# RWKV time mixing on one core: the next head pair's projections between the steps over the present pair's blocks, its last norm and new sample state beside the next pair's levels

## The chip, the cores and the metric

The kernel runs on one core of a Trainium2 chip. The metric is device time in microseconds, the median of several executions. Its core has TensorE (PE, with its weight load written PEld), VectorE (DVE), ScalarE (ACT), GpSimd (POOL) and SyncE (SP), which here issues most DMAs.

## The reference

One inference step of a two-layer trunk: an RWKV-7 layer and a convolution layer, each followed by an expert retrieval, over 512 prompt tokens and 8 samples of 8 tokens (576 columns together), width 1024, all in float32. The change is in the RWKV layer, which has 16 heads of 64 (shortened):

```python
r, k, v = jnp.einsum('ibtd,ide->ibte', xm[:3], w_rkv)
decay = jnp.exp(-jnp.exp(w));  a = jax.nn.sigmoid(a0 + (xa @ a1) @ a2);  g = jax.nn.sigmoid(xg @ g1) @ g2
kk = k * k_k;  kk = kk / jnp.maximum(jnp.sqrt(jnp.sum(kk * kk, -1, keepdims=True)), 1e-12)
def step(S, inp):
    r_t, w_t, k_t, v_t, kk_t, a_t = inp
    sa = jnp.einsum('bhij,bhj->bhi', S, -kk_t)
    S = S * w_t[:, :, None, :] + sa[..., None] * (kk_t * a_t)[:, :, None, :] + v_t[..., None] * k_t[:, :, None, :]
    return S, jnp.einsum('bhij,bhj->bhi', S, r_t)
s_fin, y = lax.scan(step, s0, xs)
yn = (y - mean) * lax.rsqrt(var + GN_EPS) * ln_w + ln_b
out = ((yn + bonus) * g) @ w_o
```

## The kernel before

The RWKV layer runs in `wkv`, a loop over C = 8 pairs of heads (i = 0 to 7, 128 channels each), with the tokens along the free axis: 4 blocks of 128 prompt tokens and 64 sample tokens. The order of each engine's instructions is written out by hand; the engines meet at counting semaphores (`Steps` gives the value at which a named step is done). A pair goes through four stages:

1. **Projections** (PE lines 418 to 440). The decay `w` and the rate `a` (expansions of hidden rows with the small weights `low2`, L412), the products for `k`, `r` and `v` with the weights in `K.w[0]`, `K.w[1]`, `K.w[2]` (L406, 16 matmuls of 288 columns each), sums for the key norm, the gate `g`, the bonus, and transposes of v, b and k to token rows (`tok_v`, `tok_b`, `tok_k`, L439). ACT evicts (L626 to L648); DVE makes the logs of decay (L704 to L715), the norm's reciprocal (L724) and the four factors at, rt, bt, kt (L730 to L735).
2. **Grams** (L447 and L465, masks on DVE L744 to L751): products of the factors within each block.
3. **Levels** (L478 to L505): the inverse of a triangular matrix of each block by six doublings. In each level PE turns the present inverse (`turn`), multiplies (`y`) and makes the correction (`dXT`); ACT evicts, and DVE adds (`XT`, L759; at the last level L761). POOL makes the factors `co` (L852) and `XT_sides` (L856).
4. **Steps** over the four blocks: for block b the rows R (L514, L517), U (L526), outputs Y (L531 to L537), state update S (L539, L540), with `update_state` on DVE (L765 to L772). Between them stand the small products of the samples (L566, L571, L547 to L559, L587, L590, L598 to L607). Then the **tail**: `mean` (L412), the samples' new state `s_S` (L615) and `var` (L412). DVE then makes the samples' new state (L819 to L823, step name `s_state`) and the last norm (reciprocal of `sd` L825, to the output rows `y` L834), in front of the next pair's logs.

SP's queue is one list as well. For each pair it loads the weights of k, r and v as their buffers come free (L372), `low2` (L374, shown by the trace as in_low) and the columns `prm` (L377), then stores the prompt's state (L382), waits for `s_state`, stores the samples' state from `s_state` (L386), waits for those stores to land and loads the next pair's into the same tile (L360):

```python
                sp.wait_ge(dve_s.sem, dve_s.before("s_state", i))
                for e in range(2):
                    q = slice(64 * e, 64 * e + 64)
                    sp.dma_start(I["o_wkv_s"][bass.ds(i - 1, 1), q].squeeze(0), s_state[q, :, q]).then_inc(stored, 16)
                sp.wait_ge(stored, i * 64 + 64)
                load_state(i)
```

After `wkv` comes `retrieval_and_conv`, the rest of the program; its first work is the product with `w_o` (L1211) whose result DVE adds to the residual `K.x` (L1607).

Of the kernel before, what the change touches and what calls it, by code (L numbers as in the profile page):

```python
# [35 lines left out]
LEVELS = 7  # L36
SLEVELS = 3
# [215 lines left out]
def wkv(nc, K, I, xm, y_out, hid_wa, hid_g, R, wo_loaded):  # L253

# [22 lines left out]
    sc = R.cut(3 * NB + SB)
    esc = R.cut(3 * NB + SB)
# [3 lines left out]
    R.cut(2, NB, HD)  # L282
    R.cut(P)
# [15 lines left out]
    Q = Region(K.arena, R.at)
    s_state = Q.cut(SB, P)  # L300
# [6 lines left out]
    Q3 = Region(K.arena, g_at)  # L307
    uv_exp = Q3.cut(SB, P)
    s_prod = Q3.cut(SB, P)
# [3 lines left out]
    stored, zeroed = K.sem("wkv_stored"), K.sem("wkv_zeroed")  # L313
    pe_s = Steps(K.sem("wkv_pe"),
                 ["w", "k", "a", "r", "norm", "v", "g", "bonus", "tok_v", "tok_b", "tok_k"]
                 + [f"gram_{x}{e}" for x in ("L", "LT", "G", "RB", "RK") for e in range(2)]
                 + [f"{x}{l}_{e}" for l in range(1, LEVELS) for step in (("turn", "y"), ("dXT",)) for e in range(2) for x in step]
                 + ["R0", "s_tok", "s_gram0", "s_gram1", "U0", "Y0", "S0"]
                 + ["s_y1", "R1", "s_d1", "U1", "Y1", "S1"]
                 + ["s_y2", "R2", "s_d2", "U2", "Y2", "S2"]  # L320
# [30 lines left out]
    with nc.Block() as block:  # L351
        @block.sync
        def _(sp):
            sp.sem_inc(stored, 64)
            weight = (1, 0, 2)

            def load_state(i):
# [1546 lines left out]
```

## Time and profile before

| | us |
|---|---|
| median of 3 runs (lowest, highest) | 3976.35 (3967.84, 3978.03) |
| the profiled execution's own time | 3980.32 |
| its span in the trace | 3978.5 |
| PE busy in the span | 2955.1 (74%) |
| DVE busy | 2732.4 (69%) |
| ACT busy | 1470.4 (37%) |
| mean granted clock of TensorE | 0.853 of full |

All times in the trace count from the span's start. A float32 matmul shows as two records, so 16 matmuls are "x32". A timeline row gives start, duration, engine, line, operation, tiles, shape, count and in brackets the engine's idle time before it with what ended it. "In pair n" below counts from 0.

### The profile page before, as it was taken

The page shows a single profiled execution, that of the slowest core. Times are in us where ns is not written, and L with a number is a line of the kernel's source. Part 1 is how long each engine was busy: PE and PEld are TensorE (multiplying, and loading weights), DVE is VectorE, ACT ScalarE, POOL GpSimd, SP SyncE. Part 2 cuts the span into 40 slices and gives each one's busy share as a digit, 9 for nine tenths or more (in the row PEclk, how much of TensorE's full clock was granted, in tenths as well). Part 3 has the DMA queues.
Part 4 walks back from the last instruction along what each step waited for, and adds up shares of the span by engine and source line. Part 5 has one row for each costly group of instructions (what it writes and reads, how often), then busy time and mean ns, then how long its engine had stood idle before and what let it go on. Part 6 is the DMA issues. An engine that isn't in the chain of part 4 may idle for free.

```text
span 3978.5 us, 56287 instructions
## 1 busy us (share of the span) xinstructions
PE 2955.1 (74%) x20248; PEld 1449.0 (36%) x20248; DVE 2732.4 (69%) x6352; ACT 1470.4 (37%) x4424; POOL 1424.2 (36%) x1272
## 2 busy tenths in 40 slices
PE   5999999868766666777777766788787676666655
PEld 3777777754222122333333322334342222222111
DVE  5555555546766666778777777889867677777775
ACT  1333333313433333444444433444444343333333
POOL 0001110014444444344444444334444444444442
PEclk8888999889787778888889888999998787787777
DMA  2110000039999999999999999999999999999996
GB/s 79 30 30 26 25 25 25 18 111 425 426 426 427 426 427 426 421 416 399 411 404 426 426 426 425 415 353 369 421 394 427 426 425 427 426 426 426 426 426 289
DMA packets 229640, 1311.06 MB, mean 330 GB/s; under 512 B 58736, under 2 KB 61936, under 8 KB 81648
## 3 DMA queue, kind: packets, MB, share of 16 engines
q0 software_dynamic: 165888, 1208.03, 72.6%
q1 hardware_dynamic: 63472, 99.43, 7.1%
q8 instruction: 159, 2.61, 0.3%
q14 instruction: 121, 0.99, 0.1%
HBM read 1301.52 MB, written 5.86 MB: 329 GB/s over the span
## 4 chain that ended last, share of the span: by engine, by line
DMA 36%; PE 19%; DVE 16%; ACT 3%; issue 3%; DVEq 1%; POOL 1%; ACTq 1%; POOLq 0%
DMA arena<-in_uv,arena 36%; DVE arena L1587 8%; PE psum L1159 8%; PE psum L1121 4%; PE psum L1211 3%; PE psum L1241 2%; DVE arena L1674 1%; POOL arena L1101 1%; ACT wbuf L1377 1%; PE psum L1231 1%; ACT arena L1372 1%; DVE arena L1515 1%; DVE arena L1512 0%; ACT arena L1368 0%; DVE arena L1648 0%
## 5 line engine op out<-in xcount | busy, mean ns | idle before, releaser
L1159 PE MATMUL psum<-arena,wbuf 64*64 64x512 f32 (+1 forms) x8704 | 1451.1, 741 | 865.7 <-ACT wbuf L1377 846.3
L1101 POOL DMA_INDIRECT arena<-in_uv,arena x1152 | 1349.7, 1172 | 1770.7 <-PE psum L1159 1569.4
L1587 DVE SCALAR_TENSOR_TENSOR arena<-arena 128x1024 f32<-128x1024 f32 x1152 | 1396.0, 1222 | 584.9 <-DMA arena<-in_uv,arena 569.6
L1159 PEld LDWEIGHTS psum<-arena,wbuf 64*64 64x64 f32 (+1 forms) x8704 | 335.0, 154 | 1755.5 <-ACT wbuf L1377 1379.3
L1368 ACT ACTIVATE arena<-arena 128x2 f32<-128x2 f32 x576 | 117.0, 203 | 1668.1 <-DVE arena L1587 1663.4
L1377 ACT ACTIVATE wbuf<-cst,arena 128x64 f32<-128x64 f32 x1152 | 338.3, 340 | 41.6 <-issue 2.4
L1121 PE MATMUL psum<-arena,wbuf 128*128 128x256 f32 (+1 forms) x1024 | 312.4, 453 | 8.5 <-DVE arena L1598 5.8
L1372 ACT ACTIVATE arena<-arena 128x1 f32<-128x1 f32 x1152 | 276.8, 287 | 40.9 <-issue 1.4
L1121 PEld LDWEIGHTS psum<-arena,wbuf 128*128 128x128 f32 x1024 | 203.9, 210 | 171.5 <-issue 131.2
L842 POOL COPY arena<-arena 128x256 f32<-128x256 f32 x8 | 3.2, 397 | 584.2 <-DVE arena L735 584.2
L406 PE MATMUL psum<-arena,wbuf 128*128 128x288 f32 x768 | 193.6, 411 | 0.4 <-DMA wbuf<-in_w_rkv 0.4
L406 PEld LDWEIGHTS psum<-arena,wbuf 128*128 128x128 f32 x768 | 145.7, 191 | 46.2 <-ACT arena L628 3.1
L1674 DVE SCALAR_TENSOR_TENSOR arena<-arena,par 128x256 f32<-128x256 f32 x240 | 115.6, 482 | 48.3 <-ACT arena L1433 42.3
L1368 ACT ACT_TABLE_LOAD x105 | 134.7, 1283 | 21.6 <-DVE arena L1587 20.0
L1231 PE MATMUL psum<-arena 128*128 128x256 f32 (+1 forms) x512 | 137.3, 415 | 0.0
L1211 PE MATMUL psum<-arena 128*128 128x320 f32 (+1 forms) x384 | 113.3, 439 | 15.6 <-ACT arena L1445 14.9
L1241 PE MATMUL psum<-arena 64*64 64x256 f32 x1024 | 121.1, 387 | 0.0
L1231 PEld LDWEIGHTS psum<-arena 128*128 128x128 f32 x512 | 93.8, 190 | 58.5 <-issue 36.5
L1358 ACT ACT_TABLE_LOAD x79 | 101.4, 1283 | 4.4 <-issue 0.3
L1211 PEld LDWEIGHTS psum<-arena 128*128 128x128 f32 x384 | 72.2, 197 | 71.2 <-issue 35.0
L1587 DVE DVE_READ_ACCUMULATOR arena<-arena 128x1 f32 x1152 | 94.3, 82 | 0.0
L1241 PEld LDWEIGHTS psum<-arena 64*64 64x64 f32 x1024 | 71.7, 137 | 55.1 <-issue 21.7
(264 smaller groups left out, 3322.9 us busy)
## 6 DMA issues: line engine op xcount, KB each, us to landing
wbuf<-in_w_q SPq DMA_DIRECT2D x64, 576.0 KB, 11.8
arena<-in_w_pw SPq DMA_DIRECT2D x48, 512.0 KB, 8.7
arena<-in_uv,arena POOLq DMA_INDIRECT x1152, 20.3
wbuf<-in_w_rkv SPq DMA_DIRECT2D x24, 512.0 KB, 3.6
wbuf<-in_w_o SPq DMA_DIRECT2D x8, 512.0 KB, 3.7
arena<-in_w_o SPq DMA_DIRECT2D x8, 512.0 KB, 8.5
x<-in_x SPq DMA_DIRECT2D x1, 2304.0 KB, 8.2
arena<-in_state SPq DMA_DIRECT2D x16, 128.0 KB, 3.0
```

Source lines behind the costliest of these rows:

```text
L406: last = pe.matmul(ps[:, bank + h, 0:HALF], w[:, k, :], src[:, k, h * HALF:(h + 1) * HALF], start=k == 0, stop=k == C - 1)
L1101: pool.indirect_dma_start(ring[:, g % RING, :], None, I["uv"][p // 2], bass.IndirectOffsetOnAxis(ap=idx[:, s % 4, j:j + 1], axis=0)).then_ ...
L1121: last = pe.matmul(ps[:, 7, 0:WIDTH[half]], K.w9[j][:, k, :], h[half][:, k, :], start=k == 0, stop=k == C - 1)
L1159: last = pe.matmul(ps[e * HD:(e + 1) * HD, 2 * (u % 2) + a if u < NB else 4, :], diag[t, g % DIAGS, :], ring[t, g % RING, D + e * 512:D + ...
L1211: last = pe.matmul(ps[:, BANK[c % 2], 0:WIDTH[half]], weights[c % 2][:, k, :], src[:, k, :], start=k == 0, stop=k == C - 1)
L1231: last = pe.matmul(out, wb[j][:, k, :], h[half][:, k, :], start=k == 0, stop=k == C - 1)
L1241: last = pe.matmul(part[q], tap_diags[q, k, :], ups[c % 2][q, k:k + 2 * P], start=k == 0, stop=k == PE_TAPS - 1)
L1368: act.activation(gelu[:, q], dots[:, q], ACT.Gelu)
L1372: act.activation(coef[:, c:c + 1], gelu[:, c:c + 1], ACT.Copy, scale=share[:, s % 4, j + k:j + k + 1])
L1377: act.activation(diag[:, (g + k) % DIAGS, :], K.ident2, ACT.Copy, scale=coef[:, c:c + 1]).then_inc(diag_ready, 1)
L1587: stt(out=row, in0=row, scalar=1.0, in1=tok[p % 2][:, UNITS[p % 2].index(u), :], op0=ALU.mult, op1=ALU.mult, accum_out=dots[:, g % COLS:g ...
L1674: last = stt(out=out, in0=up[:, k:k + 2 * P], scalar=K.par[:, TAP0 + k, c:c + 1], in1=out, op0=ALU.mult, op1=ALU.add)
```

## The change

The program's order changes in five ways; what is computed stays the same.

- PE: projections become a generator `front(n)` of 52 pieces (two of `w` and `a` together, one half of the tokens each; 48 single matmuls of k, r, v; two norm sums). Pair 0's run ahead of the loop; those of pair i+1 are handed out by `fill(count)` between the steps of pair i. All use banks 2 and 3, half by half, so evictions on ACT are split in halves too. The transposes to token rows move into levels 1 to 3.
- ACT and DVE: the next pair's evictions, exponentials, logs, rated key, norm reciprocal (in four pieces of 144 columns), bonus terms and factors stand between the present pair's steps.
- DVE: the last norm of pair i-1 and then its samples' new state are ten pieces, two of them behind each of levels 1 to 5 of pair i.
- SP: pair by pair the loads for pair i+1 (weights, `prm`, `low2`), the prompt state's store, the wait for `s_state` of pair i, the samples' store, and the load of the next samples' state.
- Several work tiles move into `K.x`; so the input x is loaded again at the end, six eighths behind the last `s_state` and two eighths behind the last `y`; the first product of the next stage waits for it.

```diff
+            for i in range(C):
+                if i < C - 1:
+                    for j, name in enumerate(("k1", "r1", "v1")):
+                        sp.wait_ge(pe_s.sem, pe_s.value(f"{name}.{i}"))
+                        sp.dma_start(K.w[j], I["w_rkv"][3 * (i + 1) + weight[j]]).then_inc(wl[j], 16)
+                    sp.wait_ge(act_s.sem, act_s.value(f"k1.{i}"))
+                    sp.wait_ge(dve_s.sem, dve_s.value(f"rk.{i}"))
+                    sp.dma_start(prm, I["cpar"][i + 1]).then_inc(prm_loaded, 16)
+                    sp.wait_ge(pe_s.sem, pe_s.value(f"g.{i}"))
+                    sp.dma_start(low2, I["low2"][i + 1]).then_inc(low_loaded, 16)
+                else:
+                    for j, name in enumerate(("k1", "r1")):
+                        sp.wait_ge(pe_s.sem, pe_s.value(f"{name}.{i}"))
+                        sp.dma_start(K.w[j], I["w_o"][j]).then_inc(wo_loaded[j], 16)
+                sp.wait_ge(dve_s.sem, dve_s.value(f"state{NB - 1}.{i}"))
...
+                sp.wait_ge(dve_s.sem, dve_s.value(f"s_state.{i}"))
+                if i == C - 1:
+                    sp.dma_start(K.x[:, 0:X_EARLY, :], I["x"][:, 0:X_EARLY, :]).then_inc(x_back, 16)
                 for e in range(2):
-                    q = slice(64 * e, 64 * e + 64)
...
+                if i < C - 1:
+                    sp.wait_ge(s_stored, i * 32 + 32)
+                    load_state(i + 1)
+            sp.wait_ge(dve_s.sem, dve_s.value(f"y.{C - 1}"))
+            sp.dma_start(K.x[:, X_EARLY:C, :], I["x"][:, X_EARLY:C, :]).then_inc(x_back, 16)
+            sp.wait_ge(p_stored, C * 32)
+            sp.wait_ge(s_stored, C * 32)
```

```diff
+            def front(n):
+
+                pe.wait_ge(low_loaded, n * 16 + 16)
                 for h in range(2):
-                    for k in range(C):
-                        last = pe.matmul(ps[:, bank + h, 0:HALF], w[:, k, :], src[:, k, h * HALF:(h + 1) * HALF],
-                                         start=k == 0, stop=k == C - 1)
-                last.then_inc(pe_s.at(name), 1)
-
-            def expand(w, src, bank, name):
+                    if h:
+                        pe.wait_ge(act_s.sem, act_s.value(f"a0.{n}"))
+                    elif n:
+                        pe.wait_ge(act_s.sem, act_s.value(f"tok_k.{n - 1}"))
+                        pe.wait_ge(dve_s.sem, dve_s.value(f"XT{LEVELS - 1}_0.{n - 1}"))
+                    pe.matmul(ps[:, 2, 0:HALF], low2[0:HD, 0, :], hid_wa[0:HD, of_half(h)], start=True, stop=True)
+                    pe.matmul(ps[:, 3, 0:HALF], low2[HD:P, 0, :], hid_wa[HD:P, of_half(h)], start=True,
+                              stop=True).then_inc(pe_s.at(f"wa{h}.{n}"), 1)
+                    yield
+                pe.wait_ge(wl[0], n * 16 + 16)
+                pe.wait_ge(act_s.sem, act_s.value(f"a1.{n}"))
                 for h in range(2):
-                    last = pe.matmul(ps[:, bank + h, 0:HALF], w, src[:, h * HALF:(h + 1) * HALF], start=True, stop=True)
-                last.then_inc(pe_s.at(name), 1)
-
+                    yield from project(n, xm[1], 0, h, "k")
+                pe.wait_ge(wl[1], n * 16 + 16)
+                pe.wait_ge(act_s.sem, act_s.value(f"k0.{n}"))
+                yield from project(n, xm[0], 1, 0, "r")
+                pe.wait_ge(act_s.sem, act_s.value(f"k1.{n}"))
...
+                yield from project(n, xm[2], 2, 0, "v")
+                pe.wait_ge(act_s.sem, act_s.value(f"r1.{n}"))
+                yield from project(n, xm[2], 2, 1, "v")
+
```

```diff
+                fill(1)
+                pe.wait_ge(act_s.sem, act_s.value(f"tok_k.{i}"))
+                pe.wait_ge(dve_s.sem, dve_s.value(f"XT{LEVELS - 1}_1.{i}"))
...
                         if j == 4:
-                            last.then_inc(pe_s.at(f"s_gram{e}"), 1)
+                            last.then_inc(pe_s.at(f"s_gram{e}.{i}"), 1)
+                fill(1)
                 rows_U(0)
+                fill(2)
                 rows_Y_S(0)
-                for b in (1, 2):
...
-                    rows_Y_S(b)
-
+                fill(6)
+                sample_y(1)
+                rows_R(1)
...
-                pe.wait_ge(act_s.sem, act_s.value("s_U", i))
-                pe.nop(nofuse=True)
+                fill(4)
+                pe.wait_ge(act_s.sem, act_s.value(f"s_U.{i}"))
                 pe.matmul(ps[:, 4, 0:NS], s_rows[NS:P, :], K.ident[NS:P, NS:P], start=True, stop=False)
```

```diff
+            def new_sample_state(i):
+                tt(s_state, s_state, s_prod, ALU.add)
+                yield
+                dve.drain()
+                tt(s_state, s_state, unsq(esc[:, i % 2, 3 * NB:3 * NB + SB], 2, P), ALU.mult).then_inc(dve_s.at(f"s_state.{i}"), 1)
+
+            def last_norm(i):
+
+                dve.wait_ge(act_s.sem, act_s.value(f"sd.{i}"))
+                for part in range(4):
+                    reciprocal(sd, part)
+                    yield
+                dve.drain()
+                tt(yc, yc, sd, ALU.mult)
+                yield
+                dve.drain()
+                ts(yc, yc, ln[:, i % 2, 0:1], ln[:, i % 2, 1:2], ALU.mult, ALU.add)
+                yield
+                dve.drain()
+                tt(yc, yc, bon[i % 2], ALU.add)
+                yield
+                dve.drain()
+                for y, t in zip(y_out, (slice(0, T // 2), slice(T // 2, N))):
+                    last = tt(y[:, i, :], yc[:, t], g_s[i % 2][:, t], ALU.mult)
+                last.then_inc(dve_s.at(f"y.{i}"), 1)
+                yield
+                yield from new_sample_state(i)
...
                         else:
-                            dve.tensor_copy(XT[0:HD, e, :, HD:P], by_block(ps[0:HD, 4 * e + 2, 0:NB * HD])).then_inc(dve_s.at(f"XT{l}_{e}"), 1)
+                            dve.tensor_copy(XT[0:HD, e, :, HD:P], by_block(ps[0:HD, 4 * e + 2, 0:NB * HD])).then_inc(dve_s.at(f"XT{l}_{e}.{i}"), 1)
+                    if l < LEVELS - 1:
+                        next(behind, None)
+                        next(behind, None)
...
+                    if n == "wA" and c in (0, X_EARLY):
+                        dve.wait_ge(x_back, 16 if c == 0 else 32)
                     dst = K.x[:, c, cols(half)]
```

On PE, the end of the levels and the start of the steps, before. L505 is the last level's `dXT`, L514 and L517 R, L566 and L571 the samples' transposes and grams, L526 U, L531 the first of Y:

```order
L505 MATMUL psum<-arena 64x64 x8
L514 MATMUL psum<-arena 128x128
L517 MATMUL psum<-arena 128x64 x2
L566 MATMUL psum<-cst,arena 128x128 x2
L571 MATMUL psum<-arena 64x64 x10
L526 MATMUL psum<-arena 128x64 x2
L531 MATMUL psum<-arena 128x128
```

The same place in pair 0 of the changed kernel. L420 and L421 are the next pair's `w` and `a`, L403 its projection matmuls, L544 the last `dXT`, L551 and L554 R, L603 and L608 the samples', L563 U, L568 the first of Y:

```order
L544 MATMUL psum<-arena 64x64 x8
L420 MATMUL psum<-arena 128x288
L421 MATMUL psum<-arena 128x288
L551 MATMUL psum<-x,arena 128x128
L554 MATMUL psum<-arena 128x64 x2
L603 MATMUL psum<-cst,x 128x128 x2
L608 MATMUL psum<-arena 64x64 x10
L420 MATMUL psum<-arena 128x288
L421 MATMUL psum<-arena 128x288
L563 MATMUL psum<-x,arena 128x64 x2
L403 MATMUL psum<-arena,wbuf 128x288 x2
L568 MATMUL psum<-arena,x 128x128
```

The next pair's first piece now stands ahead of R; behind U come the first two of its 48 projection matmuls, which before followed the whole tail.

On SP, one round of the loop before, from a pair's last loads to the next ones; in brackets the semaphores that an issue waits for:

```order
L377 DMA arena<-in_cpar 128x55 [waits wkv_dve,wkv_act]
L382 DMA out_o_wkv_p<-arena 64x64 [waits wkv_dve]
L386 DMA out_o_wkv_s<-arena 512x1x64 [waits wkv_dve]
L360 DMA arena<-in_state 64x8x64 [waits wkv_stored]
L372 DMA wbuf<-in_w_rkv 128x1024 [waits wkv_pe] x3
L374 DMA arena<-in_low 128x256 [waits wkv_pe]
```

And in the changed kernel:

```order
L376 DMA arena<-in_low 128x256 [waits wkv_pe]
L384 DMA out_o_wkv_p<-arena 64x64 [waits wkv_dve]
L390 DMA out_o_wkv_s<-arena 512x1x64 [waits wkv_dve]
L359 DMA arena<-in_state 64x8x64 [waits wkv_s_stored]
L371 DMA wbuf<-in_w_rkv 128x1024 [waits wkv_pe] x3
L374 DMA arena<-in_cpar 128x55 [waits wkv_dve,wkv_act]
L376 DMA arena<-in_low 128x256 [waits wkv_pe]
```

The order of kinds is nearly the same; the wait in front of out_o_wkv_s (`s_state` of the pair before) now ends at level 5 of the present pair, and the rows behind it carry the loads for the pair after the present one, `low2` last.

On DVE, the changed kernel's levels of pair 1. L923 is the addition `XT` of a level, L836 a quarter of the reciprocal, L874 to L884 the rest of the last norm of pair 0, L862 and L865 its samples' new state, L925 the last level's copy:

```order
L923 TENSOR_TENSOR arena<-arena,psum 128x64x2 x2
L836 RECIPROCAL x<-x 128x144 x2
L923 TENSOR_TENSOR arena<-arena,psum 128x32x4 x2
L923 TENSOR_TENSOR arena<-arena,psum 128x16x8 x2
L874 TENSOR_TENSOR x<-x 128x576
L877 TENSOR_SCALAR x<-x,arena 128x576
L880 TENSOR_TENSOR x<-x 128x576
L884 TENSOR_TENSOR arena<-x,arena 128x256
L884 TENSOR_TENSOR arena<-x,arena 128x320
L862 TENSOR_TENSOR arena<-arena,x 128x1024
L865 TENSOR_TENSOR arena<-arena 128x1024
L925 COPY arena<-psum 64x4x64 x2
```

Before, these pieces stood in one run (L821 to L834) behind the tail, beside the next pair's first projections.

## Rows read from the trace of the kernel before

**Rows 1.** Windows: stretch, length, busy PE PEld DVE ACT POOL, PEclk, DMA share, GB/s.
```profile
438.00:527.00 89.00, 80.65 (x964) 64.39 (x962) 48.59 (x95) 29.17 (x64) 9.27 (x14) 0.92 0.10 27
```

**Rows 2.** Timeline of PE, one period of the loop.
```profile
396.36 0.68 PE L478 MATMUL psum<-cst,arena 64*64 64x64 f32 x16 [0.67 <-DVE arena L751]
...
414.12 0.49 PE L514 MATMUL psum<-arena 128*128 128x128 f32 x2 [0.51 <-DVE arena L761]
...
435.80 0.41 PE L598 MATMUL psum<-arena 64*64 64x64 f32 x4 [1.94 <-DVE arena L806]
...
446.54 1.36 PE L412 MATMUL psum<-arena,cst 128*128 128x288 f32 x4
...
449.00 8.03 PE L406 MATMUL psum<-arena,wbuf 128*128 128x288 f32 x32
...
478.85 1.09 PE L439 MATMUL psum<-cst,arena 128*128 128x128 f32 x8 [1.59 <-DVE arena L735]
479.87 1.63 PE L447 MATMUL psum<-arena 64*64 64x64 f32 x80
...
485.05 0.68 PE L478 MATMUL psum<-cst,arena 64*64 64x64 f32 x16 [0.67 <-DVE arena L751]
```

**Rows 3.** Windows of 2 us, columns as in rows 1.
```profile
442.00:444.00 2.00, 2.00 (x5) 1.06 (x5) 0.87 (x2) 0.00 (x0) 0.00 (x0) 0.50 0.00 0
...
464.00:466.00 2.00, 2.00 (x10) 1.53 (x9) 0.00 (x0) 0.00 (x0) 0.00 (x0) 1.00 0.00 0
```

**Rows 4.** Timeline of SP, the end of a pair and the next pair's loads.
```profile
450.71 1.23 SPq L386 DMA_DIRECT2D out_o_wkv_s<-arena  x2
453.99 1.26 SPq L360 DMA_DIRECT2D arena<-in_state  x2
457.06 18.18 SPq L372 DMA_DIRECT2D wbuf<-in_w_rkv  x3
```

**Rows 5.** Timeline of SP, the first loads of the stage.
```profile
80.24 0.33 SPq L362 DMA_DIRECT2D arena<-in_low  x1
...
81.09 1.38 SPq L365 DMA_DIRECT2D wbuf<-in_w_rkv  x3
```

**Rows 6.** DMA view of 85 to 108 us, in 40 slices: tenths busy.
```profile
DMA  9999930000000000005778000000000010749800
```

**Rows 7.** Timeline of PE, start of the stage.
```profile
82.32 2.28 PE L412 MATMUL psum<-arena 64*128 64x288 f32 x4 [3.09 <-DMA arena<-in_low]
84.97 9.80 PE L406 MATMUL psum<-arena,wbuf 128*128 128x288 f32 x32 [0.37 <-DMA wbuf<-in_w_rkv]
```

**Rows 8.** Timeline of DVE, levels and tail.
```profile
401.84 0.29 DVE L759 TENSOR_TENSOR arena<-arena,psum 128x128 f32<-128x128 f32 x1 [2.05 <-PE psum L501]
...
413.07 0.42 DVE L761 COPY arena<-psum 64x256 f32<-64x256 f32 x1 [1.63 <-PE psum L505]
...
448.15 1.23 DVE L821 TENSOR_TENSOR arena<-arena 128x1024 f32<-128x1024 f32 x1
...
450.59 3.75 DVE L825 RECIPROCAL arena<-arena 128x576 f32<-128x576 f32 x1
```

**Rows 9.** Timeline of ACT, a table load and the work behind it.
```profile
449.15 1.28 ACT L626 ACT_TABLE_LOAD   x1 [0.47 <-PE psum L412]
450.45 0.74 ACT L626 ACTIVATE arena<-psum,arena 128x576 f32<-128x576 f32 x1
```

**Rows 10.** Timeline of PE, last pair and what follows it.
```profile
767.18 0.49 PE L514 MATMUL psum<-arena 128*128 128x128 f32 x2 [0.51 <-DVE arena L761]
...
803.10 1.13 PE L412 MATMUL psum<-arena,cst 128*128 128x288 f32 x4
814.40 9.44 PE L1211 MATMUL psum<-arena,wbuf 128*128 128x256 f32 x32 [10.17 <-PEq L351]
```

**Rows 11.** Source line L514: duration ns min/median/max, first and last start us, forms.
```profile
L514 PE MATMUL psum<-arena x64: 275/377/581, 140.5 to 789.1; 128*128 128x128 f32 x64
```

**Rows 12.** Page, DMA issues: queue, KB, us to landing.
```profile
x<-in_x SPq DMA_DIRECT2D x1, 2304.0 KB, 8.2
```

More of the change, by code:

```diff
@@ L311, in wkv @@
+    yc, ysq = Q3.cut(N), Q3.cut(N)
+    sd, s_prod = ysq, s_pick
     wl = [K.sem(f"wkv_w{j}") for j in range(3)]
     low_loaded, prm_loaded, state_loaded = (K.sem(f"wkv_{x}_loaded") for x in ("low", "prm", "state"))
[L313 to L320, printed above, removed]
-                 + ["s_RT", "R3", "U3", "s_U", "Y3", "S3"]
-                 + ["s_Y", "mean", "s_S", "var"], a_pass_ahead=True)
@@ new lines, in wkv @@
+    dve_s = Steps(K.sem("wkv_dve"), passes("logs kf kk rk factors",
+                  ["bonus"] + [f"{x}{e}" for x in ("maskLT", "level0_") for e in range(2)]
+                  + [f"gram{x}{e}" for x in ("G", "RB", "RK") for e in range(2)]
+                  + [f"XT{l}_{e}" for l in range(1, LEVELS - 2) for e in range(2)] + ["-y"]
+                  + [f"XT{LEVELS - 2}_{e}" for e in range(2)] + ["-s_state"] + [f"XT{LEVELS - 1}_{e}" for e in range(2)]
+                  + "s_gram state0 +logs s_X1 state1 +kf s_X2 state2 s_RT state3 +kk s_y s_exp +rk yc +factors s_prod".split()))
@@ L336, in wkv @@
+    pool_s = Steps(K.sem("wkv_pool"), passes("", ["s_copies"]
+                   + [f"co{l}_{e}" for l in range(1, LEVELS - 1) for e in range(2)] + ["XT_sides"]))
     assert NB == 4 and SLEVELS == 3
@@ L609, in _ @@
[L609 to L612 removed]
+                last.then_inc(pe_s.at(f"s_Y.{i}"), 1)
+                fill(4)
+                pe.wait_ge(dve_s.sem, dve_s.value(f"s_y.{i}"))
+                pe.wait_ge(act_s.sem, act_s.value(f"Y.{i}"))
+                for h in range(2):
+                    last = pe.matmul(ps[:, h, 0:HALF], K.headones, y_s[:, of_half(h)], start=True, stop=True)
@@ L613, in _ @@
+                last.then_inc(pe_s.at(f"mean.{i}"), 1)
+                for _ in ahead:
+                    pass
+                pe.wait_ge(dve_s.sem, dve_s.value(f"s_exp.{i}"))
                 for h in range(2):
@@ L693, in _ @@
+                act.wait_ge(pe_s.sem, pe_s.value(f"var.{i}"))
+                act.activation(halves(sd), of_banks(ps, 0), ACT.Sqrt, bias=K.eps[:, 1:2], scale=1.0 / HD).then_inc(act_s.at(f"sd.{i}"), 1)
         @block.vector
         def _(dve):
-            dve_s.begin(dve)
             tt, ts, stt = dve.tensor_tensor, dve.tensor_scalar, dve.scalar_tensor_tensor
@@ new lines, in _ @@
+            logs(0)
+            rated_key(0)
+            norm_floor(0)
+            for part in range(4):
+                reciprocal(nrm, part)
+            unit_key(0)
+            bonus_terms(0)
+            dve.drain()
+            make_factors(0)
+            for i in range(C):
+                n, more = i + 1, i < C - 1
+                behind = last_norm(i - 1) if i else iter(())
+                dve.wait_ge(act_s.sem, act_s.value(f"v1.{i}"))
+                dve.wait_ge(pe_s.sem, pe_s.value(f"bonus.{i}"))
+                tt(halves(bon[i % 2]), of_banks(ps, 2), halves(v_s), ALU.mult).then_inc(dve_s.at(f"bonus.{i}"), 1)
@@ L837, in _ @@
+            for _ in last_norm(C - 1):
+                pass
         @block.gpsimd
```

653 lines of the change are left out of this document (356 added, 297 removed).

## The prediction

> **What bounds the kernel now.** Read the windows by period first. In a stretch of 89 us [rows 1] TensorE is busy 80.65, VectorE 48.59, ScalarE 29.17: while `wkv` runs, PE sets the pace and no other engine is near. The rest of the program, from 814.40 on [rows 10], the change leaves alone; it is worth its old time, later or earlier by what `wkv` gives. So only the eight pairs matter.
>
> Then PE's timeline over one period [rows 2]. Levels begin at 396.36, the first R at 414.12, `var` at 446.54, and the next pair's levels at 485.05: 88.7 us, as 17.8 of levels, 33.7 of steps and tail (414.12 to about 447.8, where `var` ends and the next `w` begins), 37.2 of projections and grams. Two things cost time without PE working. First, waits: between the first R and `var` PE's timeline shows six gaps before an instruction, 0.3 to 1.94 us, 5.4 us together, the longest for the samples' rows [rows 2]; the projections' end waits 1.59 for the factors [rows 2]. Second, the clock: where projections run the granted clock is 1.00, in the tail 0.50, which is 1.2 GHz [rows 3]. In the windows of this period, 2 us each (two of 45 are shown), it is low from about 426.2 to 429.6 and 436.9 to 447.0, 13.5 us, less 1.1 us of gap. At 2.4 GHz that work takes half, 6.2 us less. So the steps' own PE work at full clock is 33.7 - 5.4 - 6.2 = 22.1 us.
>
> **The change, part by part.** I add up one period of pairs 1 to 6.
>
> Projections filled in. The three products take 8.03 us each for 16 matmuls [rows 2], 0.50 each; 24.1. Two norm sums of the same width are 1.0. The `w` and `a` pairs have 64 rows each in different halves of the array: 1.2 if they overlap, 2.3 if not; I take 1.7. Together 26.8. All of it now stands between the steps. Can the steps hide it all from waits? I walked the list with row durations. Before each thing that PE waits for stands a fill of 3 to 6 matmuls, 1.5 to 3 us, and the evictions and `update_state` (three instructions of about 0.35) take 0.3 to 1.2. For the samples' rows PE waited 1.94 behind R and U [rows 2]; now six fills, 3.0 us, stand there too. Exposed are only: `w` and `a` on ScalarE at the start, where half 1 of the expansion waits for half 0's eviction and k for both, about 1.0 with one table load (below), and 0.5 before `mean` and at the next pair, where DVE's list (uv_exp, bonus terms, then five factor products) is tightest. Steps and tail: 22.1 + 26.8 + 1.5 = 50.4. Bounds 48.5 (overlap, no wait) and 52.5 (one more microsecond of each).
>
> The table load is 1.28, and the activation behind it starts 1.30 after it [rows 9]; so a switch costs 1.3 here. The Trainium skill ("ScalarE: Activation LUTs", What ACT_TABLE_LOAD costs) says that a switch to another set takes about 2.66 us, a drain of 1.38 included. By that, an estimate, the first wait of each steps stage would be 1.4 longer, and the whole some 10 us slower; the trace disagrees, with no such gap before the activation.
>
> Gate, bonus and grams. 1.0 + 1.0 + the stretch from L447 to the levels, 485.05 - 479.87 = 5.2 [rows 2], + 0.3 of waiting for `s_prod`: 7.5.
>
> Levels. 17.1 from 396.36 to where DVE's copy L761 ends, 413.07 + 0.42 [rows 2, 8]. Plus the three transposes, 0.5 each, 1.5. Plus DVE's pieces: each level leaves it 2.05 idle [rows 8]. A quarter of the 3.75 reciprocal [rows 8] is 0.94, two are 1.9; the next pairs of pieces are 1.5 and 1.75; these fit. Behind level 5 stand two passes of 1024 columns, 1.23 each [rows 8], 2.6 with the drain between, in a gap of 1.63 [rows 8]: 1.0 longer. Sum 19.6.
>
> SP's queue, the new wait. This is the term that decides. In the order of SP, the loads of weights, `prm` and `low2` for pair i+1 stand behind the samples' store and load, and these behind `s_state` of pair i-1, which DVE now makes behind level 5 of pair i. Call that moment S. The store is issued at once and the state load follows 3.28 later (450.71 to 453.99, [rows 4]), as it waits for landing; two issues take 1.26 [rows 4]; so the first weights go out at S + 4.6. At the start of the stage three weights go out from 81.09 [rows 5], and the queue is busy until 88.05 (five and a third slices of 0.575 from 85, [rows 6]), the state's 256 KB included: 6.96 us. Now the state's bytes lead and `low2` ends the queue, so it lands near S + 11.5. PE's `front` asks for it right behind the last level, when DVE has made the first copy, S + 0.6. PE therefore stands 10.9 us, with R, U and everything of the steps queued behind the waiting instruction; ACT stands before `prm` as well. If `low2` didn't queue behind the weights it would need only its own issue, S + 6.5, and the 2.1 from 80.24 to the first matmul at 82.32 [rows 5, 7]: 8.0 us of stall. Upper bound 11.4. The case occurs for i = 1 to 6; pair 0 has no `s_state` ahead of its loads, pair 7 no next pair.
>
> The clock after the stall. At the start of the stage PE had waited 3.09; its first expansion took 2.28 and k 9.80 [rows 7] against 8.03 at full clock [rows 2]: 1.1 + 1.8 = 2.9 lost. Here the first microseconds hold waits for ACT anyway, so I take 2.2, bounds 0 and 4.0.
>
> Sum per period: 50.4 + 7.5 + 19.6 + 10.9 + 2.2 = 90.6, where before had 88.7. Without the last two terms it would be 77.5.
>
> The whole. Pair 0's R began at 140.5 [rows 11]. Its projections lose about 1.5 to finer waits and save the 1.6 and the transposes; the transposes return in the levels: 141.2. Steps of pair 0 without stall: 191.6. Six periods: 543.6, so 735.2. Pair 7: 7.5 + 19.6 + 0.6 to its R, 762.9, before 767.18 [rows 10]. Its steps have no fills: 33.7 as in rows 2, or 37.0 as pair 7 took (767.18 to 803.10 + 1.13, [rows 10]); 35.3 gives 798.2, before 804.2.
>
> Then the end. Before, PE went on at 814.40 [rows 10], 10.2 behind `var`, when DVE was through the last norm. Now that norm no longer waits for the samples' state and ends 8.2 behind `var` (0.9 for `sd`, 3.9 for the reciprocal, 3.4 for five further passes), `s_state` follows 2.6 later, and only then SP sends six eighths of x, 1.77 MB, ahead of the samples' store whose landing closes the stage. The whole x took 8.2 [rows 12]; six eighths about 6.7. With the store behind it some 8.6: 19.4 behind `var`, 9.2 more than before. So the next stage begins at 817.6 instead of 814.4: 3.2 on top of the profiled execution's own 3980.32 (span 3978.5), or 0.1%. That execution lies 4 above the median 3976.35 of the runs, so the median to expect is 3979.5, which I give as 3979: **no change that can be told**. I call 0.3%, 12 us, the bound of that.
>
> **The rivals.**
> 1. *A shorter stall.* `low2` and k's weights land early, 8.0 instead of 10.9, and the clock is back sooner (1.0 lost): -4.1 x 6 = -25, 3954. For it: most loads land in 3.6 us alone. Against: the start shows three weights filling the queue for 7 us [rows 5, 6]. It also stands for steps at their low bound, 48.5: -13.
> 2. *No stall*, as if the loads were early enough: 77.5 a period, -79, 3900. It takes SP to pass a wait that stands in its list; nothing speaks for that but a slip of my reading.
> 3. *Slower: the clock stays at 1.2 GHz.* After each stall the steps stage begins with its thinnest PE work, and before, a low stretch lasted from 436.9 to 447.0 though PE was busy [rows 3]. Each further microsecond at half clock in the filled steps costs 0.5. Up to 6 us low is in my sum; it decides from 9 us low on (1.5 x 6 = 9, with the 3 above), and at 12 us gives +18, 3997. Against: k reached full clock within a few us at the start [rows 7]. The Trainium skill ("TensorE: Matmul & The Clock Gate", Why this matters for your kernels) has it that idle gaps between bursts send the array back to half rate, and steady work restores it; it speaks for the loss after each of the six stalls, and not for a longer one.
>
> **How the numbers follow.** Forecast case 0.42; rival 1 0.24; rival 2 0.08; rival 3, with DVE or ACT chains that run over, 0.26. Per period the bounds (8.0 to 11.4, 48.5 to 52.5, 0 to 4.0) would together give -42 to +26 us; eight in ten I put at 3936 to 4001, leaving out rival 2 and the far ends. Faster by over 0.3%: rivals 1 and 2, 0.32. Slower by over 0.3%: rival 3 and the forecast's upper edge, 0.29. Within: 0.39.
>
> **What would show it.** In the changed kernel's trace: PE idle about 11 us before L420 in pairs 1 to 6, ended by the load of in_low, and no such gap in pair 0; granted clock 0.5 right behind it; then a steps stage of 50 us nearly without gaps at 1.00; SP's weights issued 4.6 behind L865; some 9 us more between last `var` and the first product of the next stage. The prediction fails if that gap is under 8 us, if the filled steps take over 53, or if the clock falls within them.

## The result, and the profile after the change

| us | before | after |
|---|---|---|
| median of 10 runs (lowest, highest) | 3974.70 (3967.84, 3978.03) | 3981.18 (3978.09, 3987.98) |
| span of the profiled execution | 3978.5 | 3978.4 |
| PE, DVE, ACT busy in it | 2955.1, 2732.4, 1470.4 | 2913.3, 2732.4, 1471.2 |
| mean granted clock | 0.853 | 0.859 |

After over before is 1.0019, 95% interval 1.0011 to 1.0028: 0.2% slower. That is within the 0.3% called no change, and 3981 is 2 us from the 3979 forecast. The step itself is 6.5 us where 3.2 were forecast, but so small a step says little: the median of the kernel before was 3976.6 and 3978.2 when it was measured again beside the experiments. The order of a whole stage has changed and the sum has not. Two things must be shown: what the fills saved, and what took it back.

Start with how often a pair comes round. SP stores the prompt's state once a pair. Its timeline in the changed kernel (start, duration, queue and line):

```profile
181.34 1.18 SPq L384 DMA_DIRECT2D out_o_wkv_p<-arena  x2
...
722.68 1.16 SPq L384 DMA_DIRECT2D out_o_wkv_p<-arena  x2
```

From first to last are six periods, (722.68 - 181.34) / 6 = 90.22 us, of the forecast 90.6. The window of one period (columns as in [rows 1]):

```profile
438.00:527.00 89.00, 75.11 (x960) 59.85 (x959) 48.51 (x101) 27.94 (x68) 10.19 (x14) 0.92 0.10 27
```

PE is now busy 75.11 of 89 where it was 80.65 [rows 1], with nearly the same number of matmuls (960 records for 964) and the same mean clock of 0.92. So there is a hole of some 12 us, part of the low clock lies in it, and what work there is goes faster. PE's timeline of one period, which answers to [rows 2], shows it. L544 is the last level's `dXT`, L420 the next pair's `w`, L403 its products, L472 the gate, L508 the start of the levels, L457 transposes to token rows:

```profile
396.11 1.25 PE L544 MATMUL psum<-arena 64*64 64x64 f32 x16
409.65 0.84 PE L420 MATMUL psum<-arena 64*128 64x288 f32 x1 [12.29 <-DMA arena<-in_low]
...
416.49 2.26 PE L403 MATMUL psum<-arena,wbuf 128*128 128x288 f32 x4
...
462.49 1.13 PE L472 MATMUL psum<-arena 128*128 128x288 f32 x4
...
469.54 0.68 PE L508 MATMUL psum<-cst,arena 64*64 64x64 f32 x16 [0.51 <-DVE arena L914]
...
471.53 0.66 PE L457 MATMUL psum<-cst,arena 128*128 128x128 f32 x4
...
475.15 0.66 PE L457 MATMUL psum<-cst,arena 128*128 128x128 f32 x4
...
487.65 1.25 PE L544 MATMUL psum<-arena 64*64 64x64 f32 x16
501.48 0.84 PE L420 MATMUL psum<-arena 64*128 64x288 f32 x1 [12.58 <-DMA arena<-in_low]
```

One gap of 12.29 us between the end of the levels and the first piece of the next projections, ended by the load of low2. The steps after it have 48 projection matmuls among them and up to the gate one wait, of 0.30. The view of waits, 82 to 830 us (engine, line, what was waited for: total, times, longest), says how often:

```profile
PE psum L420 <- DMA arena<-in_low: 78.1, 7, 12.9
```

Seven times: 3.00 at the start of the stage, then once for each of pairs 1 to 6, 75.1 us in all, 12.5 each. What low2 waited for stands in SP's timeline, the answer to [rows 4]:

```profile
397.91 1.23 SPq L390 DMA_DIRECT2D out_o_wkv_s<-arena  x2
401.16 1.26 SPq L359 DMA_DIRECT2D arena<-in_state  x2
402.47 1.57 SPq L371 DMA_DIRECT2D wbuf<-in_w_rkv  x3
404.13 0.38 SPq L374 DMA_DIRECT2D arena<-in_cpar  x1
404.55 0.60 SPq L376 DMA_DIRECT2D arena<-in_low  x1
```

and in DVE's, at the same place (L865 is the second pass of the samples' new state, step `s_state`; L925 the last level's copies):

```profile
396.40 1.48 DVE L865 TENSOR_TENSOR arena<-arena 128x1024 f32<-128x1024 f32 x1
397.81 0.73 DVE L925 COPY arena<-psum 64x256 f32<-64x256 f32 x2
```

`s_state` is done at 396.40 + 1.48 = 397.88 and SP's store goes out at 397.91. Store, wait for landing, state load, then three weights, `prm`, and low2 as the last at 404.55. All of that is for a pair whose first matmul was due at 398. PE starts at 409.65.

The clock behind the gap, in windows of 2 us as in [rows 3]:

```profile
402.00:404.00 2.00, 0.00 (x0) 0.00 (x0) 0.00 (x0) 0.00 (x0) 0.00 (x0) 0.50 0.53 120
...
418.00:420.00 2.00, 2.00 (x12) 1.40 (x10) 0.00 (x0) 0.00 (x0) 0.00 (x0) 0.50 0.00 0
430.00:432.00 2.00, 2.00 (x14) 1.64 (x11) 0.99 (x3) 0.18 (x1) 0.00 (x0) 1.00 0.00 0
```

0.50 of full, which is 1.2 GHz, from within the gap to 420, and then 1.00 through steps and tail, where before it was 0.50 for 13.5 us. The six pairs are not alike in this. In windows of 1 us the clock is low until 4 to 6 us behind the first `w` in four of them, and until 10.4 behind it in two, the one shown here and the one that starts at 590.63.

The end of `wkv`, PE and then SP, as in [rows 10]:

```profile
796.73 1.13 PE L675 MATMUL psum<-x,cst 128*128 128x288 f32 x4
817.24 9.87 PE L1377 MATMUL psum<-arena,wbuf 128*128 128x256 f32 x32 [19.38 <-PEq L351]
```

```profile
808.15 0.33 SPq L387 DMA_DIRECT2D x<-in_x  x1
808.53 1.68 SPq L390 DMA_DIRECT2D out_o_wkv_s<-arena  x2
```

19.38 idle behind `var` instead of 10.17; x is reloaded behind the last samples' state, and the store stands behind that load (experiment 3 tests it). Of the pairs' gain nothing is left there either: the next stage starts at 817.24, 2.8 later than before.

### The profile page after: what moved, and what is told of

The parts are those of the page before. It is cut to its first block, busy times and chain, and to the rows that moved or that the text cites. A ratio compares the mean times of both kernels' runs of the same rounds, so it can differ in the third digit from the quotient of the medians.

```text
span 3978.4 us, 56329 instructions
## 1 busy us (share of the span) xinstructions
PE 2913.3 (73%) x20248; PEld 1416.6 (36%) x20248; DVE 2732.4 (69%) x6400; ACT 1471.2 (37%) x4472; POOL 1413.2 (36%) x1272
## 4 chain that ended last, share of the span: by engine, by line
DMA 35%; PE 18%; DVE 17%; ACT 3%; issue 3%; DVEq 1%; POOL 1%; ACTq 1%; POOLq 0%
DMA arena<-in_uv,arena 35%; DVE arena L1753 9%; PE psum L1325 8%; PE psum L1377 3%; PE psum L1287 3%; PE psum L1407 2%; DVE arena L1842 1%; POOL arena L1267 1%; ACT wbuf L1543 1%; PE psum L1397 1%; ACT arena L1538 1%; DVE arena L1681 1%; DVE arena L1678 1%; DVE arena L1685 0%; DVE level L1707 0%
## 5 line engine op out<-in xcount | busy, mean ns | idle before, releaser
L1267 POOL DMA_INDIRECT arena<-in_uv,arena x1152 | 1333.0, 1157 | 1785.2 <-PE psum L1325 1578.3
L1287 PE MATMUL psum<-arena,wbuf 128*128 128x256 f32 (+1 forms) x1024 | 304.4, 444 | 8.4 <-DVE arena L1764 5.8
L1287 PEld LDWEIGHTS psum<-arena,wbuf 128*128 128x128 f32 x1024 | 198.5, 204 | 166.9 <-issue 127.3
L403 PE MATMUL psum<-arena,wbuf 128*128 128x288 f32 x768 | 212.2, 419 | 4.6 <-ACT arena L683 3.6
L403 PEld LDWEIGHTS psum<-arena,wbuf 128*128 128x128 f32 x768 | 141.2, 194 | 41.3 <-issue 5.3
```

Source lines behind the costliest of these rows:

```text
L403: last = pe.matmul(ps[:, 2 + h, 0:HALF], K.w[j][:, k, :], src[:, k, of_half(h)], start=k == 0, stop=k == C - 1)
L1267: pool.indirect_dma_start(ring[:, g % RING, :], None, I["uv"][p // 2], bass.IndirectOffsetOnAxis(ap=idx[:, s % 4, j:j + 1], axis=0)).then_ ...
L1287: last = pe.matmul(ps[:, 7, 0:WIDTH[half]], K.w9[j][:, k, :], h[half][:, k, :], start=k == 0, stop=k == C - 1)
```

## The experiments

Theory A is the forecast's: the fills are worth about 13 us a pair, and SP's list, in which the loads of the next pair stand behind the wait for `s_state`, takes the same back. The main rival B: the order on PE itself is no better, and low2's wait only takes up time that PE, DVE or ACT would lose anyway; without it another wait would come out. Rival C: not the queue's wait but the amount of loads ahead of low2 counts. And for the clock: half clock behind the gap is a cost of its own (D), or hidden by waits for ACT. All kernels compute the reference in full; junk matmuls below are matmuls whose result nobody reads.

**1. The loads ahead of the wait (e1_queue).** SP issues the loads for the pair after next before it waits for `s_state`.

```diff
+            next_loads(0)
+            for i in range(C):
                 sp.wait_ge(dve_s.sem, dve_s.value(f"state{NB - 1}.{i}"))
...
+                if i < C - 1:
+                    next_loads(i + 1)
                 sp.wait_ge(dve_s.sem, dve_s.value(f"s_state.{i}"))
```

> Edit: on SP the loads for pair i+2 (weights, prm, low2) stand ahead of the wait for s_state of pair i, not behind it. Theory A (the queue order makes the six stalls): the six gaps of about 12 us before the expansion of w and a are gone, and with them some 2 us each of half clock; 6 x 13 = 78 us less than the changed kernel's 3981, 3903, ratio to before 0.982. Theory B (the filled steps themselves have eaten the gain, and the gap would only move to another wait): 3970 or more, with a new gap of like size in the steps.

Measured 3906.94 (3897.16 to 3912.35), ratio 0.983 [0.9814, 0.9847]. The same part of SP's timeline:

```profile
333.45 1.15 SPq L387 DMA_DIRECT2D out_o_wkv_p<-arena  x2
334.64 6.63 SPq L371 DMA_DIRECT2D wbuf<-in_w_rkv  x3
...
344.60 0.33 SPq L376 DMA_DIRECT2D arena<-in_low  x1
370.39 1.24 SPq L395 DMA_DIRECT2D out_o_wkv_s<-arena  x2
```

low2 is issued at 344.60, 26 us before it is wanted. PE there:

```profile
370.84 0.82 PE L425 MATMUL psum<-arena 64*128 64x288 f32 x1 [0.99 <-DVE arena L930]
```

The gap before `w` (L425 now) is 0.99, ended by DVE, instead of 12.3 ended by a load. Three of the six periods between prompt stores are 76.65 (180.15, 256.80, 333.45), the others 77.6, 77.6 and 80.2, mean 77.54; the forecast's sum without stall and low clock was 77.5. Before, the mean was 89.3, so the gain is 11.8 a pair, and 12.7 where the clock stays up. The next stage starts at 733.18, 84 earlier; the ratios of the medians show 75 of them, as the profiled execution (3897.16) was the fastest of the four. That is A; B would have kept the time. In the longer periods the clock is what differs. Two windows of the longest, behind the 0.99 gap above:

```profile
370.00:382.00 12.00, 11.12 (x59) 7.99 (x60) 3.85 (x22) 3.79 (x8) 0.85 (x1) 0.57 0.22 44
382.00:394.00 12.00, 12.00 (x74) 9.27 (x72) 6.03 (x18) 2.70 (x9) 0.00 (x0) 1.00 0.01 2
```

12 us at 0.57, with no gap over a microsecond. The window from 260 to 349 us of this kernel, mostly in periods of 76.65, is at 1.00.

**2. Only the order of the loads (e2_small_first).** They stay behind the wait; `prm` and low2 go ahead of the three weights.

```diff
+                    sp.dma_start(prm, I["cpar"][i + 1]).then_inc(prm_loaded, 16)
+                    sp.wait_ge(pe_s.sem, pe_s.value(f"g.{i}"))
+                    sp.dma_start(low2, I["low2"][i + 1]).then_inc(low_loaded, 16)
+                    for j, name in enumerate(("k1", "r1", "v1")):
```

> Edit: only the order of the loads behind s_state is changed: prm and low2 ahead of the three weights. If low2 is late because 1.5 MB of weights stand ahead of it in the queue: it lands near S + 7 instead of S + 11.7, each gap shrinks by 4.5 to 5 us, the k product isn't held up by its weights (they land near S + 10, it is wanted near S + 13), 3981 - 28 = 3953. If the landing is set by the issue alone, weights or not: within 5 us of 3981. If PE then only waits for the weights of k instead: also near 3981, with a gap before the first projection matmul.

3959.86 (3957.92 to 3963.81), ratio 0.9957 [0.9941, 0.9974]. SP and PE:

```profile
393.95 1.23 SPq L390 DMA_DIRECT2D out_o_wkv_s<-arena  x2
...
399.17 0.43 SPq L373 DMA_DIRECT2D arena<-in_low  x1
399.64 1.38 SPq L376 DMA_DIRECT2D wbuf<-in_w_rkv  x3
```

```profile
402.19 0.84 PE L420 MATMUL psum<-arena 64*128 64x288 f32 x1 [8.79 <-DMA arena<-in_low]
...
409.03 1.30 PE L403 MATMUL psum<-arena,wbuf 128*128 128x288 f32 x2
```

In this pair low2 goes out 5.2 behind `s_state` instead of 6.7, and PE starts 8.2 behind it instead of 11.8. Over the six pairs PE's idle time before `w` is 8.65 on average instead of 12.52: 3.9 less, of the 4.5 expected; some 0.5 of it is lost again to a longer low clock (first `w` to the gate takes 51.8 instead of 51.3). The weights don't hold up k (L403 at 409.03 has no wait). So C holds for three tenths of the stall; the rest is the wait itself with store and state load.

**3. The end of the stage (e3_store_first).** e1, and the last pair's sample store goes ahead of x.

```diff
+                if i == C - 1:
+                    sp.dma_start(K.x[:, 0:X_EARLY, :], I["x"][:, 0:X_EARLY, :]).then_inc(x_back[0], 16)
```

This now stands behind the two stores of L390, with a semaphore for each part of x.

> e1 plus, for the last pair, the samples' store issued ahead of the reload of x, with a semaphore of its own for each part of x. Theory (the stage's end waits for a store queued behind 1.77 MB of x): the next stage's first product starts some 4 to 5 us earlier behind the last var than in e1, DVE's first addition to x isn't held up; 4 us less than e1. Rival (the reload is then waited for by the first addition to x instead): same time as e1.

3901.57 (3897.56 to 3902.0), ratio 0.9813 [0.9796, 0.9829], against e1 in the same rounds 5.4 less. With four runs of e1 spread over 15 us the medians alone can't carry that; the gap in the trace does. PE at the end, first of e1, then of e3:

```profile
733.18 7.05 PE L1382 MATMUL psum<-arena,wbuf 128*128 128x256 f32 x25 [19.34 <-PEq L351]
```

```profile
721.05 1.13 PE L680 MATMUL psum<-x,cst 128*128 128x288 f32 x4
736.43 4.17 PE L1382 MATMUL psum<-arena,wbuf 128*128 128x256 f32 x9 [14.25 <-PEq L351]
```

19.34 idle becomes 14.25. The forecast's reading of the end was right: the store's landing closed the stage, and it stood behind 1.77 MB of x. The next stage itself starts no earlier in this one execution (736.43 for 733.18), since the last pair, which has no fills, took longer: its prompt store comes 70.9 behind the one before it, where in e1 it was 60.8, with the clock low for most of 682 to 720 us.

**4. The samples' second pass one level later (e4_level6).** e3, with the two passes of 1024 columns behind levels 5 and 6 in place of both behind 5.

```diff
-                    if l < LEVELS - 1:
+                    next(behind, None)
+                    if l < LEVELS - 2:
                         next(behind, None)
```

> e3 plus the second pass of the samples' new state moved from behind level 5 to behind level 6. My term: the two passes behind level 5 make the last level 1.0 us longer in pairs 1 to 7; with one of them away, 7 x 1.0 = 7 us less than e3. Rival: the second pass then delays the samples' grams on DVE, which the fills on PE cover or not: 0.

3884.07 (3883.73 to 3884.92), ratio 0.9769 [0.9753, 0.9785]. Every period is 75.68: 0.97 less than 76.65, which is the term "DVE passes behind level 5, 1.0" of the forecast. But the whole is 17.5 below e3, with 7 expected. A window, and PE behind the levels:

```profile
438.00:527.00 89.00, 86.03 (x1170) 69.23 (x1167) 56.96 (x130) 34.37 (x85) 11.43 (x16) 1.00 0.13 33
```

```profile
443.61 0.48 PE L425 MATMUL psum<-arena 64*128 64x288 f32 x1
...
448.53 1.21 PE L408 MATMUL psum<-arena,wbuf 128*128 128x288 f32 x4 [0.50 <-ACT arena L688]
```

No gap is left before `w`, and the clock is 1.00 in the windows from 171 to 616 us throughout. Between the starts of the next stage (736.43, 721.39) lie 15.0. The six periods are 9.1 shorter, 5.8 of it the passes and 3.3 e3's longer periods, those with low clock; another 5.5 lie in the last pair (65.4 for 70.9), the rest at the start. The median's 17.5 is 2.5 more, and the profiled spans (3895.8, 3882.0) differ by 13.8: what lies behind `wkv` varies by a few microseconds either way. That part isn't settled.

The short gap and the low clock go together. In e1 and e3, with a gap of 0.99 or 1.00 before each first `w` of pairs 1 to 6, the clock fell behind it in six of twelve steps stages, for 3 to 4 us in five and for about 10 in one. In e4, and in e7 and e9 which are built on it, without that gap, it fell in none of 18.

**5. The clock in the kernel before (e5_idle).** The order of before, with 10 junk matmuls (some 3 us) in four of PE's waits in each pair's steps and tail.

```diff
                 for b in (1, 2):
+                    idle(1, 3, 2 * P, 2 * P)
                     sample_y(b)
...
+                idle(6, 3, 3 * P, P)
                 pe.wait_ge(dve_s.sem, dve_s.value("s_RT", i))
...
+                idle(2, 5, 0, 2 * P)
                 pe.wait_ge(dve_s.sem, dve_s.value("s_y", i))
```

Each multiplies `K.ident` with 128 or 256 columns.

> The kernel before, with junk matmuls (identity by a piece of xm, into PSUM columns that are written again later) put on PE in front of its waits in the steps: one of 256 columns before each of the samples' two y products, six of 128 before the wait for the samples' rows, two of 256 before the wait for y: 3.0 us of work a pair at full clock, where PE stands 4 us. The output is the same. Theory (the low clock of the steps and tail, 6.2 us a pair, comes from PE's gaps): part of the low stretches goes, 3 to 5 us a pair less, 24 to 40 us, 3940 to 3950. Rival (the clock falls for the thin matmuls, gaps or not): no gain, 0 to 10 us slower, as the junk overruns some waits.

3934.79 (3928.28 to 3936.82), ratio 0.9882 [0.9864, 0.9899]: 43 us less for adding work.

```profile
438.00:527.00 89.00, 83.32 (x996) 66.55 (x995) 48.98 (x96) 28.99 (x63) 9.27 (x14) 0.98 0.10 27
```

The clock is 0.98 where before had 0.92 [rows 1]. Prompt stores come every 84.8 instead of 89.3. So low clock cost the kernel before at least 4.6 us a pair, of the 6.2 that the forecast took off the steps; and four tenths of what the fills are worth once their loads are on time (11.8 a pair) is had by this alone. Of the whole time it is more, 43 us against e1's 70 below the kernel before.

**6. Busy through the stall (e6_busy_stall, e8_busy25).** The changed kernel, with 22 (25) junk matmuls ahead of the piece that waits for low2.

```diff
+                if 0 < i < C - 1:
+                    pe.wait_ge(act_s.sem, act_s.value(f"tok_k.{i}"))
+                    for _ in range(22):
+                        pe.matmul(ps[:, 3, 0:HALF], K.ident, xm[0][:, 0, 0:HALF], start=True, stop=True)
```

> The changed kernel, with 22 junk matmuls of 288 columns (11 us at full clock, into a bank that is written again) on PE ahead of the next pair's first piece in pairs 1 to 6, so that PE works while it would wait for low2. The output is the same. If my clock term is right (2.2 us a stall, because PE restarts at half rate): the stall itself stays to within a microsecond, the steps behind it start at 2.4 GHz, 6 x 2.2 = 13 us less, 3968. If the clock behind the stall costs nothing (lower bound 0): 3981. If as much as the upper bound, 4.0: 3957.

> e6 with 25 junk matmuls in place of 22, 12.4 us, as long as the stall, since in e6 PE still stood 3.3 us behind the junk and fell to half clock again. If the clock's part of a stall is 2.2 us (the period of the changed kernel less that of e1, 13.5, less the extra idle before L420, 11.3): 13 us less than the changed kernel, 3968, period 88.0. If it is what e6 gave back, 1.05: 3975.

With 22: 3974.58 (3969.2 to 3978.72), ratio 0.9992 [0.9982, 1.0001]. With 25: 3972.33 (3967.91 to 3977.64 in nine executions; the tenth took 4409.99 at a mean clock of 0.626, unexplained), ratio 0.9989 [0.9979, 0.9999]. The medians are 6.6 and 8.9 below the changed kernel's 3981.18, of the 13 that D would give; by the ratios to the kernel before, each taken in its own rounds, it is 11 and 12. PE in e6, its windows (the gap, and just behind it), and PE in e8, with the gate (L472) at the end of a steps stage:

```profile
395.94 10.94 PE L600 MATMUL psum<-arena,cst 128*128 128x288 f32 x44
410.14 0.51 PE L420 MATMUL psum<-arena 64*128 64x288 f32 x1 [3.26 <-DMA arena<-in_low]
...
415.96 1.21 PE L403 MATMUL psum<-arena,wbuf 128*128 128x288 f32 x4 [0.49 <-ACT arena L687]
```

```profile
408.00:410.00 2.00, 0.00 (x0) 0.00 (x0) 0.00 (x0) 0.00 (x0) 0.00 (x0) 1.00 0.64 235
...
412.00:414.00 2.00, 2.00 (x24) 1.60 (x24) 0.35 (x3) 1.60 (x5) 0.00 (x0) 0.50 0.00 0
```

```profile
408.31 0.51 PE L420 MATMUL psum<-arena 64*128 64x288 f32 x1 [1.79 <-DMA arena<-in_low]
...
497.59 0.51 PE L420 MATMUL psum<-arena 64*128 64x288 f32 x1 [0.40 <-DMA arena<-in_low]
...
546.85 1.13 PE L472 MATMUL psum<-arena 128*128 128x288 f32 x4
```

The first `w` runs at full clock (0.51; in after 0.84). But 3.26 us of idle were left, and from 412 the clock is low after all, behind work at full rate; from this `w` to k are 5.82 instead of 6.84. In e6 that happens in three of the six pairs, in e8 in one, with 1.79 left.

From first `w` to the gate the six pairs of e8 take 49.26 five times (546.85 less 497.59 is one) and 50.15 once, mean 49.4; e6 has 49.7, after 51.3. So with PE kept busy the steps are 1.9 us shorter, and that is D with nearly its full size. Why the period shows less, 89.17 (e6) and 88.88 (e8), only 1.05 and 1.34 below after: the first `w` starts 12.55 behind the end of `s_state` instead of 12.0, so 0.55 a pair of stall came on top. What made low2 land later isn't shown.

**7. The last pair (e7_last_pair, e9_last_busy).** e4, and for the last pair the samples' new state ahead of the last norm; then junk matmuls in the last pair's waits, where there are no fills, and 20 behind `var`.

```diff
                 yield
-                yield from new_sample_state(i)
+                if i < C - 1:
+                    yield from new_sample_state(i)
...
             dve.drain()
+            for _ in new_sample_state(C - 1):
+                pass
             for _ in last_norm(C - 1):
```

```diff
+                def idle(count):
+                    for _ in range(count if i == C - 1 else 0):
+                        pe.matmul(ps[:, 3, 0:HALF], K.ident, xm[0][:, 0, 0:HALF], start=True, stop=True)
...
                 last.then_inc(pe_s.at(f"var.{i}"), 1)
+                idle(20)
```

> e4 with the last pair's new sample state ahead of its last norm, so that the samples' store and six eighths of x leave SP 8 us earlier, beside the norm. The stage then ends with the norm, 8.2 + 2.6 = 10.8 us behind the last var, where e3 and e4 end some 14.5 behind: 3.5 us less than e4 in the trace by the start of the next stage's first product. In the medians that is 0.1%, at the edge of what they tell. Rival: the first addition to x then waits for the reload: no gain.

> e7 with junk matmuls of 288 columns on PE in the last pair only, whose steps have no projections to fill them: 1, 1, 3 and 2 ahead of its four waits, and 20 behind var, beside the last norm. Output the same. If the low clock there comes from PE's gaps, as e5 showed for the kernel before: the last pair's steps take 3 to 4 us less and the next stage's first product 7.2 instead of 9.4; 6 us less than e7, 3876. If not: 3882 or a little more.

e7 3881.88 (3879.79 to 3883.95), ratio 0.9754 [0.9738, 0.977], a step of 2 us from e4 that the runs don't tell apart; e9 3872.83 (3870.46 to 3875.06), ratio **0.9739 [0.9722, 0.9755]**, the best of all. The first products of the next stage, e7 and then e9:

```profile
718.61 9.40 PE L1385 MATMUL psum<-arena,wbuf 128*128 128x256 f32 x32 [10.81 <-PEq L351]
```

```profile
700.86 9.86 PE L476 MATMUL psum<-arena,cst 128*128 128x288 f32 x40
711.83 7.14 PE L1394 MATMUL psum<-arena,wbuf 128*128 128x256 f32 x32 [1.11 <-PEq L351]
```

e7's gap is 10.81, 3.5 less than 14.27 in e4: the store and six eighths of x no longer wait for the norm, and the last part of x, issued at 717.73 behind `y`, closes the stage. In e9 the products (L1394) start 6.8 earlier, 4.9 of it from the last pair's steps (the last prompt store at 695.29 instead of 700.20), and take 7.14 instead of 9.40 as PE comes to them from work. The ranges of e7 and e9 don't overlap, so the 9 us are real. How much of the 4.9 is the junk's isn't settled by one trace each: from the last but one prompt store to the last it is 65.3 in e7 and 60.1 in e9, but 60.8 in e1, which has no junk, and 70.9 in e3.

## Why the forecast held, step by step

- **Steps with fills, 50.4, and clock 2.2.** From first `w` to the gate, six times: 51.03, 50.33, 52.84, 50.36, 52.80, 50.41, mean 51.3 against 52.6. In e1 (76.65, less 7.05 and 19.36 from the rows above, less 0.99 of gap) the same stretch is 49.25, and e8 has 49.26 behind a stall. So the steps are 1.1 shorter than forecast, and the clock takes 2.05 behind a stall. The waits were sized rightly: in e1 they are 0.56 and 0.49 on ScalarE at the start and 0.30 at `mean`, 1.35 for the forecast's 1.5. The `w` and `a` pairs take 0.68 each, 1.36 instead of 1.7; where the other 0.65 lies isn't shown. The 2.2 of clock was partly luck: four of the six periods lost 1.1 to 1.8 and two lost 3.6, with the clock low until 10.4 us behind the first `w`. The Trainium skill ("TensorE: Matmul & The Clock Gate", Why this matters for your kernels) says that idle gaps between bursts send PE back to half rate; the trace agrees, with 0.50 in all six gaps and behind them.
- **Table load, 1.30.** ACT behind the stall:

```profile
411.07 1.28 ACT L682 ACT_TABLE_LOAD   x1 [14.44 <-PE psum L421]
412.37 0.50 ACT L682 ACTIVATE arena<-psum,arena 128x288 f32<-128x288 f32 x1
```

The activation starts 1.30 after the load, as in [rows 9]; the 2.66 that the Trainium skill gives ("ScalarE: Activation LUTs", What ACT_TABLE_LOAD costs) isn't seen here, nor where ScalarE comes to the load straight from work (L705, load at 432.64, activation at 433.94).

- **Gate, bonus, grams, 7.5.** 7.05 (462.49 to 469.54).
- **Levels, 19.6.** 20.5 (469.54 to the end of DVE's copies, 489.35 + 0.74, the same step as the copies at 397.81). The step that was mis-sized: a round of transposes makes a level 3.62 long (471.53 to 475.15) where it was 2.92, so 0.7 each and not 0.5; and the second state pass took 1.48, not 1.23. The part called 1.0 measured 0.97 in e4.
- **Stall, 10.9.** 11.3: 12.5 of PE's idle time less 1.2 in which DVE finishes. Low2 lands a little later than estimated, about 12.0 behind `s_state` on average instead of 11.5. Its two causes are shown apart: e1 takes all of it away, e2 the 3.9 for the weights ahead.
- **Sum.** 51.3 + 7.05 + 19.36 + 12.52 = 90.2 by PE's own ends, for 90.6. Of the terms, steps came out 1.15 lower, gate, bonus and grams 0.45 and the clock 0.15 lower, levels 0.9 and the stall 0.4 higher. That the sum is within 0.4 owes something to these signs.
- **Whole and end.** Pair 0's steps end at 191.33 (191.6 forecast), pair 7's R at 760.41 (762.9), end of `var` 797.86 (798.2), 19.38 behind it (19.4), next stage 817.24 (817.6). That is 2.8 behind before; the median is 6.5 behind. The profiled spans are equal, so the remaining 3.6 can't be placed by these traces. That the end of `var` agrees within 0.4 is in part luck: the six periods came out 2.3 shorter than forecast, and pair 7's steps, put at 35.3, took 37.45, close to the 37.0 that pair 7 had before.
- **Rivals.** Rival 1 fell with the stall, 11.3 and not 8.0. Rival 2 is e1. Rival 3 came true in part: in two of the six periods the clock was low past its limit of 9 us behind the stall, which made these two some 2.3 longer than the other four, where it was low about half as long.

So the large change had a large gain, 11.8 us a pair, and paid it back as one new wait in a queue that was moved past the thing it waits for.

## What to carry to other kernels

When work is moved ahead of other work, move its loads ahead in the issuing engine's list as well, and read that list for every wait that stands before them: here one of them was worth 1.9% of the whole. Within the list put what is small and wanted first ahead of what is big and wanted later. Where PE must wait for a microsecond or more again and again, look at the granted clock behind it; matmuls that nobody reads are cheap to try there.

## What was unexpected of the hardware

- Added matmuls alone made the kernel before 1.2% faster (e5), with the clock of a period up from 0.92 to 0.98.
- Half clock came behind short gaps too: in e1 12 us at 0.57 behind 0.99 us of idle, in other periods of the same kernel none; over e1 and e3 six times of twelve, and never in 18 steps stages without that gap. In e6 it came 0.5 to 1.5 us after work had begun again at full rate. The length of the gap doesn't decide it alone: in e6 the clock fell behind 1.89 us of idle and not behind 2.34. What does isn't known from these runs.
